# First weights and tables of five stages loaded in the stage before them, or by a second queue

## The chip, the core and the metric

The kernel runs on one core of a Trainium2 chip. All times are device microseconds of one execution; the time of a kernel is the median of several executions. Tensors are float32. The engines of the core are TensorE (PE in the rows; its weight loads are PEld), VectorE (DVE), ScalarE (ACT), GpSimd (POOL) and SyncE (SP). Transfers are issued by SP's queue, by ScalarE's (ACTq) and by GpSimd's; they run on 16 transfer engines.

## What is computed

One layer of a diffusion backbone over 2048 latent tokens of width 1024, with a context of 256 tokens ahead of them. Cut to what the change touches:

```python
h = rmsnorm(x) * (1 + sc1) + sh1
p = h @ w_in                                     # 1024 x N_IN
ya, _, _ = deltanet_branch(p[:, :A_COLS], ...)   # recurrence over chunks, two directions
x0, x1, v = split(short_conv(p[:, B_OFF:C_OFF]) + b)          # Hyena, 256 wide each
z = x1 * v
yb = x0 * (irfft(rfft(z, 4096) * rfft(kern, 4096))[:2048] + z * bias)
yc = B * short_conv(C * hx)                                   # from p[:, C_OFF:G_OFF]
gates = sigmoid(p[:, G_OFF:])                                 # 3 x 1024
merged = gates[0] * (ya @ w_branch_a) + gates[1] * (yb @ w_branch_b) + gates[2] * (yc @ w_branch_c)
x = x + g1 * (merged @ w_out)                                 # then norm, routing to experts, final norm
```

## The kernel before

The program is a chain of stages. Each is one `nc.Block()` with a list of instructions for each engine, and between two blocks all engines meet at a barrier; within a block they meet by semaphores (`then_inc`, `wait_ge`), and each engine takes its list in order. A transfer adds 16 to its semaphore when it has landed. Buffers that a stage allocates with `sbt(st, ...)` are given back at its end, so the next stage's buffers lie in the same bytes and can't be filled before the barrier. `recycle()` clears all semaphores and adds one more barrier. Between 685 and 1295 us runs the recurrence (DN here, block of line 1124); the stages behind it are those of the change:

- **H** (block of line 1543): projections and short convolutions of Hyena and of the short branch. Twelve quads `q` take a weight block `raw[:, q % 2]` (`raw_h`, 1024 KB, loaded by `load_raw`) and multiply it with half of `hT` in seven products of four matrices each (Winograd's form of a 2 x 2 product): line 1589, in the order `p1`, `p5`, `u2`, `c11`, `u3`, `c12`, `c21`. VectorE makes the sums of weights (`s1` to `s4`) and of tokens (`t1` to `t4`), ScalarE keeps intermediate results (`p1s`, `p5s`, `u2s`: `kept`, line 1655). Beside them ScalarE scales tiles of `ada_w` (`scale_tiles`, line 1661) and GpSimd adds them up (line 1879); six of these tiles come ahead of `p1s` in quad 0. SP issues `load_raw(0)`, `load_raw(1)`, ten rows of a few KB, and then the `ada_w` tiles (line 1556). `z` goes to memory as `z_d`; the filter `h_d` was written in the first stage.
- **A** (block of line 1896): first step of the transform. For 16 blocks of four columns SP loads four pieces `hb` (filters, 64 KB) and four `zb` (signal, 32 KB), up to four blocks ahead; TensorE multiplies with the table `fw`; VectorE copies to `az` (two buffers, 66 partitions), ScalarE's queue stores three parts of 264 KB to `fa_d`, and VectorE waits for these stores (`a_st`) before it fills the buffer again. SP loads `fw` in two parts, of 528 KB (behind block 0) and 1584 KB.
- **C** (block of line 1975): second step, products of the spectra and the inverse step. Eleven blocks `sp_in` (two buffers, six pieces of 192 KB each, reloaded when the block two earlier is used up); 22 parts, each with products by the matrices `gm` 0 and 1 (lines 2023, 2024, part `s = 0` of the block only), 2 to 5 (lines 2027 to 2030, parts 1 and 2) and 6 (line 2013). In between the recurrence's outputs are read (`load_o`, 512 KB a tile), added and normalised. Results go to `fb_d`.
- **D** (block of line 2127): last step. 16 blocks `bb` (two transfers of 132 KB, 66 rows) times the table `fd` (66 rows, 528 KB); both buffers have 128 partitions, and VectorE and GpSimd set the rows from 64 on to zero before the transfers may write. Each block is followed by four transposes of `yaT` (line 2168).
- **Y** (block of line 2209): y is loaded as `yn` (four transfers of 512 KB), transposed on TensorE, and multiplied on VectorE and GpSimd.
- **W** (block of line 2277): gates and branch products. 24 quads of the same seven products (line 2314), with weights `raw_w` (1024 KB a quad) and `bw` (1024 KB in three parts, used one quad later).

## Time and profile before

| | |
|---|---|
| time, median of 3 (us) | 4042.16 (4040.48 to 4047.41) |
| profiled execution: time, span (us) | 4042.21, 4040.4 |
| TensorE busy | 3744.9 us, 93% |
| VectorE, ScalarE, GpSimd busy | 48%, 27%, 22% |
| bytes moved | 384 MB read, 111 MB written, mean 122 GB/s |

The span is that of the profile, from the first to the last instruction; the time of the same execution is 1.8 us longer. In rows with a duration the first number is the start in us from the span's start, the second the length; brackets hold the idle time of the engine ahead of the row and what ended it. A row may join instructions of the same kind that follow one another (`x8`); a float32 matrix product shows as two records. The share of a transfer row and the clock are means over the stretch; the clock is 1.00 at 2.4 GHz and 0.50 at 1.2 GHz.

### The profile page before, as it was taken

To read this page: it belongs to the slowest core of one execution; us is meant where nothing else is said; L and a number is where in the kernel's file an instruction comes from. 1 tells how busy PE (TensorE), PEld (TensorE's weight loads), DVE (VectorE), ACT (ScalarE), POOL (GpSimd) and SP (SyncE) were. 2 spreads that over 40 slices of the span, in tenths; PEclk is the share of its full clock that TensorE was granted. 3 is DMA by queue.
4 is the path that set the end of the run, shared out by engine and by line. 5 is a ranking of instruction groups with operands and counts; after the bars stand their busy time and mean duration, and the time that the engine had idled before them with its cause. 6 is when DMAs were issued, how large, how long until landed. Compare 5 with 4: busy or idle time off the path is not lost. (4 is left out here: it accounts for less than half of the span.)

```text
span 4040.4 us, 46896 instructions
## 1 busy us (share of the span) xinstructions
PE 3744.9 (93%) x17200; PEld 2401.5 (59%) x17200; DVE 1942.1 (48%) x2964; ACT 1101.5 (27%) x2313; POOL 900.5 (22%) x661
## 2 busy tenths in 40 slices
PE   6999998999998999887999999997976999999997
PEld 2854444888887444344344444443546888888885
DVE  4344544555555743635322222224435666666667
ACT  4155555444444511031111111111210111111113
POOL 1012222333333700031011111111331222122224
PEclk8699999999999999988999999998977999999998
DMA  7122333222222511695111111105442655665565
GB/s 267 35 76 76 89 94 98 71 78 78 78 78 82 181 54 42 199 238 167 57 53 54 52 54 58 55 27 195 140 174 84 215 189 202 207 213 193 192 218 210
DMA packets 297697, 497.25 MB, mean 123 GB/s; under 512 B 21447, under 2 KB 176746, under 8 KB 297204
## 3 DMA queue, kind: packets, MB, share of 16 engines
q1 hardware_dynamic: 277601, 431.65, 32.3%
q0 software_dynamic: 12096, 43.84, 4.1%
q10 hardware_dynamic: 7829, 19.46, 1.5%
q8 instruction: 110, 1.80, 0.2%
q14 instruction: 61, 0.50, 0.0%
HBM read 384.11 MB, written 110.77 MB: 122 GB/s over the span
## 5 line engine op out<-in xcount | busy, mean ns | idle before, releaser
L2314 PE MATMUL bank<-hT,raw_w 128*128 128x512 f32 x576 | 260.6, 595 | 9.5 <-DMA raw_w<-in_w_in 9.5
L3343 PEld LDWEIGHTS bank<-xeT,raw_e 128*128 128x128 f32 x2304 | 263.6, 192 | 7.2 <-issue 7.2
L3343 PE MATMUL bank<-xeT,raw_e 128*128 128x128 f32 x2304 | 267.8, 275 | 0.0
L2506 POOL TENSOR_TENSOR mg<-mg,sg_m 128x512 f32<-128x512 f32 x64 | 88.1, 1377 | 719.3 <-DVE sg_m L2408 719.3
L887 POOL TENSOR_SCALAR sg<-tmp 128x512 f32<-128x512 f32 (+1 forms) x76 | 111.9, 1473 | 469.1 <-DVE tmp L955 413.9
L2314 PEld LDWEIGHTS bank<-hT,raw_w 128*128 128x128 f32 x576 | 110.0, 191 | 148.0 <-issue 138.2
L3343 PE MATMUL bank<-T_e,U 128*128 128x128 f32 x1536 | 176.7, 275 | 0.0
L664 PE MATMUL bank<-T_d,S_d 128*128 128x512 f32 x384 | 174.1, 603 | 0.0
L3343 PEld LDWEIGHTS bank<-T_e,U 128*128 128x128 f32 x1536 | 174.1, 192 | 0.0
L2314 PE MATMUL bank<-zT,S 128*128 128x512 f32 x384 | 172.6, 592 | 0.0
L2408 DVE TENSOR_TENSOR sg_m<-sg_m,bank 128x512 f32<-128x512 f32 x64 | 43.9, 686 | 242.2 <-PE bank L2326 242.2
L2377 ACT ACTIVATE sg_m<-sg_m 128x512 f32<-128x512 f32 x72 | 45.4, 630 | 395.3 <-DVE sg_m L2417 395.3
L1211 PE MATMUL bank<-T,Nc 128*128 128x128 f32 x864 | 137.1, 281 | 15.0 <-DVE T L1411 11.9
L1221 PE MATMUL bank<-E,TTm 128*128 128x128 f32 x864 | 146.5, 294 | 0.3
L1434 DVE TENSOR_TENSOR E<-bank,lv 128x256 f32<-128x256 f32 x216 | 91.6, 424 | 82.6 <-PE bank L1211 82.1
L1221 PEld LDWEIGHTS bank<-E,TTm 128*128 128x128 f32 x864 | 113.4, 191 | 27.0 <-issue 3.0
L3349 PE MATMUL bank<-raw_e,hid_e 128*128 128x512 f32 x288 | 128.9, 592 | 0.0
L2314 PEld LDWEIGHTS bank<-zT,S 128*128 128x128 f32 x384 | 73.0, 190 | 91.8 <-issue 91.8
L1211 PEld LDWEIGHTS bank<-T,Nc 128*128 128x128 f32 x864 | 114.5, 192 | 20.9 <-issue 17.9
L664 PEld LDWEIGHTS bank<-T_d,S_d 128*128 128x128 f32 x384 | 73.9, 195 | 89.3 <-issue 89.3
L1295 ACT ACTIVATE Tq<-T 128x256 f32<-128x256 f32 x216 | 89.1, 420 | 122.3 <-DVE T L1443 73.6
L664 PE MATMUL bank<-hT,raw_d 128*128 128x512 f32 x256 | 118.2, 605 | 0.0
(509 smaller groups left out, 7641.1 us busy)
## 6 DMA issues: line engine op xcount, KB each, us to landing
raw_e<-in_exp_w_gate SPq DMA_DIRECT2D x16, 3072.0 KB
raw_e<-in_exp_w_up SPq DMA_DIRECT2D x16, 3072.0 KB
raw_e<-in_exp_w_down SPq DMA_DIRECT2D x16, 3072.0 KB
raw_w<-in_w_in SPq DMA_DIRECT2D x24, 1024.0 KB, 5.3
raw_d<-in_w_in SPq DMA_DIRECT2D x16, 1024.0 KB, 5.9
fa_d<-az ACTq DMA_DIRECT2D x48, 264.0 KB
sp_in<-fa_d SPq DMA_DIRECT2D x66, 192.0 KB, 5.2
raw_h<-in_w_in SPq DMA_DIRECT2D x12, 1024.0 KB, 5.3
```

Source lines behind the costliest of these rows:

```text
L664: mm = pe.matmul(bank[:, :], lhs[:, k, :], rhs[:, k, :], start=first and k == 0, stop=k == 3, skip_group_check=not first)
L887: pool.tensor_scalar_max(sg[:, g % TB, 0:w], tmp[:, g % TB, 0:w], CLAMP).then_inc(clamp_ok, 1)
L1211: last = pe.matmul(b4(x)[:, h % 2, :], Nc[:, h, :], mixed(T, b, h, 1, 0), start=True, stop=True)
L1221: last = pe.matmul(b4(2 + x)[:, h % 2, :], TTm[:, h, :], E1[:, h, :], start=True, stop=True)
L1295: act.activation(Tq[:, 2 * x:2 * x + 2, :].rearrange("p h (n t b) -> p (h n) t b", t=2, b=b), mixed(T, b, 2 * x, 2, 1), ACT.Copy).then_inc ...
L1434: dve.tensor_tensor(E1[:, 2 * x:2 * x + 2, :], b4(x)[:, 0:2, :], lv[:, l, :].unsqueeze(1).to_broadcast([P, 2, P]), ALU.mult).then_inc(P_ok, 1)
L2314: mm = pe.matmul(bank[:, :], lhs[:, k, :], rhs[:, k, :], start=first and k == 0, stop=k == 3, skip_group_check=not first)
L2377: act.activation(sg[:, i, :], src, ACT.Sigmoid).then_inc(sg_ok[i], 1)
L2408: dve.tensor_tensor(dst, sg[:, i, :], O(q, i)[:, :], ALU.mult).then_inc(pr_ok[i], 1)
L2506: pool.tensor_tensor(mg[:, i, :], mg[:, i, :], sg[:, i, :], ALU.add).then_inc(add_ok[i], 1)
L3343: mm = pe.matmul(bank[:, f * P:(f + 1) * P], lhs[:, k, f * P:(f + 1) * P], rhs[:, k, :], start=fresh and k == 0, stop=k == 3, skip_group_c ...
L3349: mm = pe.matmul(bank[:, :], lhs[:, f, :], rhs[:, f, :], start=first and f == 0, stop=f == HF - 1, skip_group_check=not first)
```

## The change

- `raw_h` is allocated at the other end of SBUF (`side="right"`), ahead of DN, and its two first loads are issued in DN, behind the first eight keys, queries and values; SP waits for them at DN's end. The waits of quads 0 and 1 go, those of later quads count one load less.
- In A the first part of `fw` and the four `hb` pieces of block 0 are issued by ScalarE's queue; SP begins with `zb`. The table `gm` (448 KB), allocated at the other end, is loaded in A, behind the second part of `fw`, and SP waits for it at A's end.
- In C the pieces `s = 0` of a block keep the semaphore `s_in`, the four others get `hz_in`, for which TensorE waits between lines 2024 and 2027.
- In D `bb` and `fd` have 66 partitions, the memsets and their semaphore are gone, and `fd` is issued by ScalarE's queue.
- `raw_w` and `bw` are allocated at the other end ahead of Y, and the first two loads of `raw_w` and the first three of `bw` are issued in Y behind `yn`.

```diff
@@ -1064,6 +1064,11 @@
+        far = lambda stack, name, shape: stack.enter_context(nc.sbuf_tensor(name, shape, F32, side="right"))
+        hst = top.enter_context(ExitStack())
+        raw_h = far(hst, "raw_h", [P, 2, KD, 2 * P])
+        raw_h_in = sem("raw_h_in")
+
         with ExitStack() as st:
             NL = len(LEVELS)
             lv, pair = sbt(st, "lv", [P, NL, P]), sbt(st, "pair", [P, P])
@@ -1136,6 +1141,9 @@
                             sp.dma_start(pair[:, :], A["t_pair"]).then_inc(lv_in, 16)
                     for e in range(4):
                         load(0, e, values, ldv)
+                    for q in range(2):
+                        c0 = B_OFF + q * HW
+                        sp.dma_start(raw_h[:, q], A["w_in"][0, :, c0:c0 + HW].rearrange("(k p) c -> p k c", p=P)).then_inc(raw_h_in, 16)
                     def step(it, w, inverse, more):
                         es = (2 * w, 2 * w + 1)
@@ -1151,6 +1159,7 @@
                                 load(it, e + 4, values, ldv)
                     all_steps(sp, step)
+                    sp.wait_ge(raw_h_in, 32)
                     for q in range(4):
                         sp.wait_ge(o_st[q], 16 * (STEPS // 2 + 1))
@@ -1478,7 +1487,8 @@
         with ExitStack() as st:
-            raw, S1, S2, S4 = sbt(st, "raw_h", [P, 2, KD, 2 * P]), *[sbt(st, n, [P, 4, P]) for n in ("S1_h", "S2_h", "S4_h")]
+            raw = raw_h
+            S1, S2, S4 = [sbt(st, n, [P, 4, P]) for n in ("S1_h", "S2_h", "S4_h")]
@@ -1555,8 +1565,6 @@
                             b, k = divmod(t, KD)
                             sp.dma_start(md[t % RM], A["ada_w"][0, k * P:(k + 1) * P, 2 * D + b * 512:2 * D + (b + 1) * 512]).then_inc(md_in[t % RM], 16)
-                    load_raw(0)
-                    load_raw(1)
                     for b in range(NMOD):
                         sp.dma_start(mod_row(b), A["ada_b"][:, 2 * D + b * 512:2 * D + (b + 1) * 512]).then_inc(n2_in, 16)
                     for b in (4, 5):
@@ -1608,7 +1616,8 @@
                     for q in range(NQ):
                         p, kind = quads[q]
-                        pe.wait_ge(raw_in[q % 2], 16 * (q // 2 + 1))
+                        if q >= 2:
+                            pe.wait_ge(raw_in[q % 2], 16 * (q // 2))
                         if q >= 2:
                             pe.wait_ge(x_free, q - 1)
                         product(X(q), w(q, 0, 0), t(p, 0, 0), True).then_inc(p1_mm, 1)
@@ -1782,7 +1791,8 @@
                             dve.sem_inc(x_free, 1)
                     def s1(q):
-                        dve.wait_ge(raw_in[q % 2], 16 * (q // 2 + 1))
+                        if q >= 2:
+                            dve.wait_ge(raw_in[q % 2], 16 * (q // 2))
                         if q >= 1:
                             dve.wait_ge(p5_mm, q)
                         dve.tensor_tensor(S1[:, :, :], w(q, 1, 0), w(q, 1, 1), ALU.add).then_inc(s1_ok, 1)
@@ -1886,6 +1896,10 @@
         EV = NB + NB // 2
         NBLK = FN // NB
         RB = 4
+        hst.close()
+        mst = top.enter_context(ExitStack())
+        gm = far(mst, "gm", [P, 7, P])
+        g_in = sem("g_in")
         with ExitStack() as st:
             fw = sbt(st, "fw", [P, NBLK, NB, 2 * FK])
             zb = sbt(st, "zb", [P, RB, HW])
@@ -1899,13 +1913,13 @@
                     for i in range(NBLK):
                         if i >= RB:
                             sp.wait_ge(a_mm, (i - RB + 1) * EV)
-                        for buf, src in ((hb, h_d), (zb, z_d)):
+                        for buf, src in ((hb, h_d), (zb, z_d)) if i else ((zb, z_d),):
                             for n in range(NB):
                                 sp.dma_start(buf[n * FR:(n + 1) * FR, i % RB], src.rearrange("(a n) c -> n a c", n=FN)[i * NB + n]).then_inc(b_in[i % RB], 16)
-                        if i == 0:
-                            sp.dma_start(fw[:, 0:RB], A["t_fa"][:, 0:RB]).then_inc(fw_in[0], 16)
                         if i == 1:
                             sp.dma_start(fw[:, RB:NBLK], A["t_fa"][:, RB:NBLK]).then_inc(fw_in[1], 16)
+                            sp.dma_start(gm[:, :, :], A["t_g"]).then_inc(g_in, 16)
+                    sp.wait_ge(g_in, 16)
                 @block.tensor
                 def _(pe):
@@ -1940,6 +1954,9 @@
                 @block.scalar
                 def _(act):
+                    act.dma_start(fw[:, 0:RB], A["t_fa"][:, 0:RB]).then_inc(fw_in[0], 16)
+                    for n in range(NB):
+                        act.dma_start(hb[n * FR:(n + 1) * FR, 0], h_d.rearrange("(a n) c -> n a c", n=FN)[n]).then_inc(b_in[0], 16)
                     for i in range(NBLK):
                         act.wait_ge(a_ev, (i + 1) * EV)
                         for s in range(3):
@@ -1960,13 +1977,12 @@
         own = lambda t: yaT[:, :, t * P:(t + 1) * P]
         with ExitStack() as st:
-            gm = sbt(st, "gm", [P, 7, P])
             sp_in = sbt(st, "sp_in", [P, 2, 3, 3, HW])
             xs = sbt(st, "xs", [P, 2, 2, CW])
             yp = sbt(st, "yp", [P, 2, 2, CW])
             bk = sbt(st, "bk", [P, 2, CW])
             obb, sqb, ss = sbt(st, "obb", [P, 4, HEADS, P]), sbt(st, "sqb", [P, 2, HEADS, P]), sbt(st, "ss_o", [P, TILES, HEADS])
-            g_in, s_in = sem("g_in"), [sem("s_in0"), sem("s_in1")]
+            s_in, hz_in = [sem("s_in0"), sem("s_in1")], [sem("hz_in0"), sem("hz_in1")]
             BLOCKS = FK // 3
@@ -1989,9 +2005,8 @@
                             sp.wait_ge(sx_mm, 4 * n - 4)
                         for s in range(3):
                             for r in range(2):
-                                sp.dma_start(sp_in[r * FN:(r + 1) * FN, n % 2, s], fa_d[s, r, 3 * n:3 * n + 3, :, :].rearrange("k n c -> n k c")).then_inc(s_in[n % 2], 16)
-
-                    sp.dma_start(gm[:, :, :], A["t_g"]).then_inc(g_in, 16)
+                                sp.dma_start(sp_in[r * FN:(r + 1) * FN, n % 2, s], fa_d[s, r, 3 * n:3 * n + 3, :, :].rearrange("k n c -> n k c")).then_inc((hz_in if s else s_in)[n % 2], 16)
+
                     load_block(0)
                     load_o(0)
                     load_block(1)
@@ -2012,16 +2027,17 @@
                             pe.wait_ge(c_cp, m - 1)
                         pe.matmul(PS[6 + m % 2][:, 0:CW], gm[:, 6, :], yp[:, m % 2, 0, :], start=True, stop=True).then_inc(c_mm, 1)
-                    pe.wait_ge(g_in, 16)
                     for m in range(PARTS):
                         n, v = m // 2, m % 2
                         if v == 0:
-                            pe.wait_ge(s_in[n % 2], 96 * (n // 2 + 1))
+                            pe.wait_ge(s_in[n % 2], 32 * (n // 2 + 1))
                         sig = [sp_in[:, n % 2, s].rearrange("p k c -> p (k c)")[:, v * CW:(v + 1) * CW] for s in range(3)]
                         if m >= 1:
                             pe.wait_ge(sx_cp, 2 * m)
                         pe.matmul(PS[0][:, 0:CW], gm[:, 0, :], sig[0], start=True, stop=True)
                         pe.matmul(PS[1][:, 0:CW], gm[:, 1, :], sig[0], start=True, stop=True).then_inc(sx_mm, 1)
+                        if v == 0:
+                            pe.wait_ge(hz_in[n % 2], 64 * (n // 2 + 1))
                         if m >= 2:
                             pe.wait_ge(sp_pr, 2 * m - 2)
                         pe.matmul(PS[2 + 2 * v][:, 0:CW], gm[:, 2, :], sig[1], start=True, stop=False)
@@ -2111,16 +2127,17 @@
                         if 0 <= t < TILES:
                             pool.wait_ge(o_in[t % 4], 32 * (t // 4 + 1))
                             pool.tensor_tensor(own(t), own(t), obb[:, t % 4], ALU.add).then_inc(sum_ok, 1)
+        mst.close()
         if stop == 9:
             return
         with ExitStack() as st:
             RD = 4
-            bb = sbt(st, "bb", [P, RD, NB, HW])
-            fd = sbt(st, "fd", [P, FN, FR])
+            bb = sbt(st, "bb", [2 * FK, RD, NB, HW])
+            fd = sbt(st, "fd", [2 * FK, FN, FR])
             ys = sbt(st, "ys", [FR, 2, NB, HW])
-            pad_ok, fd_in = sem("pad_ok"), sem("fd_in")
+            fd_in = sem("fd_in")
             o_tr, ya_ok = sem("o_tr"), sem("ya_ok")
             BE = NB // 2
@@ -2133,10 +2150,7 @@
                         for r in range(2):
                             sp.dma_start(bb[r * FK:(r + 1) * FK, i % RD], fb_d[r, i * NB:(i + 1) * NB, :, :].rearrange("n k c -> k n c")).then_inc(d_in[i % RD], 16)
-                    sp.wait_ge(pad_ok, 1)
                     load(0)
-                    sp.wait_ge(pad_ok, 2)
-                    sp.dma_start(fd[0:2 * FK], A["t_fd"]).then_inc(fd_in, 16)
                     for i in range(1, RD):
                         load(i)
                     for i in range(NBLK):
@@ -2170,7 +2184,6 @@
                 @block.vector
                 def _(dve):
-                    dve.memset(bb[64:P, :, :, :], 0.0).then_inc(pad_ok, 1)
                     for i in range(NBLK):
                         b = i % 2
                         if i >= 2:
@@ -2185,13 +2198,9 @@
                             dve.scalar_tensor_tensor(own(i), PS[4 + i % 4][:, :].rearrange("p (h t) -> p h t", t=P),
                                                      cols[:, R_NG:R_NG + 1], szb[:, i % 4], ALU.mult, ALU.mult).then_inc(ya_ok, 1)
-                @block.gpsimd
-                def _(pool):
-                    pool.wait_ge(pad_ok, 1)
-                    pool.memset(fd[64:P, :, :], 0.0).then_inc(pad_ok, 1)
-
                 @block.scalar
                 def _(act):
+                    act.dma_start(fd[:, :, :], A["t_fd"]).then_inc(fd_in, 16)
                     for i in range(NBLK):
                         act.wait_ge(d_ev, (i + 1) * BE)
                         act.dma_start(y_d.rearrange("(a n) c -> a n c", n=FN)[:, i * NB:(i + 1) * NB, :], ys[:, i % 2]).then_inc(d_st[i % 2], 16)
@@ -2203,6 +2212,10 @@
         ost.close()
         recycle()
+        wst = top.enter_context(ExitStack())
+        raw_w, bw = far(wst, "raw_w", [P, 2, KD, 2 * P]), far(wst, "bw", [P, KD, 2 * P])
+        raw_in, bw_in = [sem("raw_in0"), sem("raw_in1")], [sem(f"bw_in{j}") for j in range(3)]
+        branch_weights = [(0, 4, "w_branch_a"), (4, 2, "w_branch_b"), (6, 2, "w_branch_c")]
         with ExitStack() as st:
             yn, ty = sbt(st, "yn", [P, NT, 4, HW]), sbt(st, "ty", [P, 2 * NT, TW])
             y_in, y_tr, y_ok, y_own = [sem(f"y_in{g}") for g in range(NT)], sem("y_tr"), sem("yt_ok"), sem("y_own")
@@ -2211,6 +2224,11 @@
                 def _(sp):
                     for g in range(NT):
                         sp.dma_start(yn[:, g], y_d[g * TW:(g + 1) * TW, :].rearrange("(j p) c -> p j c", p=P)).then_inc(y_in[g], 16)
+                    for q in range(2):
+                        c0 = G_OFF + q * D
+                        sp.dma_start(raw_w[:, q], A["w_in"][0, :, c0:c0 + 2 * P].rearrange("(k p) c -> p k c", p=P)).then_inc(raw_in[q], 16)
+                    for q, (k0, nk, name) in enumerate(branch_weights):
+                        sp.dma_start(bw[:, k0:k0 + nk, :], A[name][0, :, 0:2 * P].rearrange("(k p) c -> p k c", p=P)).then_inc(bw_in[q], 16)
                 @block.tensor
                 def _(pe):
@@ -2245,13 +2263,13 @@
         with ExitStack() as st:
-            raw, S1, S2, S4 = sbt(st, "raw_w", [P, 2, KD, 2 * P]), *[sbt(st, n, [P, 4, P]) for n in ("S1", "S2", "S4")]
+            raw = raw_w
+            S1, S2, S4 = [sbt(st, n, [P, 4, P]) for n in ("S1", "S2", "S4")]
             T1, T2 = [zT[:, x, :].rearrange("p (k t) -> p k t", t=TW) for x in range(2)]
             T4 = sbt(st, "T4", [P, 4, TW])
-            bw = sbt(st, "bw", [P, KD, 2 * P])
             p1s, p5s, u2s = [sbt(st, n, [P, TW]) for n in ("p1s", "p5s", "u2s")]
             sg, mg = sbt(st, "sg_m", [P, 4, TW]), sbt(st, "mg", [P, 4, TW])
-            raw_in, bw_in, mg_st = [sem("raw_in0"), sem("raw_in1")], [sem(f"bw_in{j}") for j in range(3)], [sem(f"mg_st{i}") for i in range(4)]
+            mg_st = [sem(f"mg_st{i}") for i in range(4)]
             s1_ok, s2_ok, s3_ok, s4_ok = [sem(n) for n in ("s1_ok", "s2_ok", "s3_ok", "s4_ok")]
             t1_ok, t2_ok, t3_ok, t4_ok = [sem(n) for n in ("t1_ok", "t2_ok", "t3_ok", "t4_ok")]
@@ -2287,10 +2305,6 @@
                         _, k0, nk, name = branch[j]
                         sp.dma_start(bw[:, k0:k0 + nk, :], A[name][0, :, cp * 2 * P:(cp + 1) * 2 * P].rearrange("(k p) c -> p k c", p=P)).then_inc(bw_in[j], 16)
-                    load_raw(0)
-                    load_raw(1)
-                    for q in range(3):
-                        load_bw(q)
                     for q in range(1, NQ + 1):
                         p, cp, j = quads[q - 1]
                         if q + 1 < NQ:
@@ -2504,6 +2518,7 @@
                         for i in range(4):
                             pool.wait_ge(pr_ok[i], q + 1)
                             pool.tensor_tensor(mg[:, i, :], mg[:, i, :], sg[:, i, :], ALU.add).then_inc(add_ok[i], 1)
+        wst.close()
         if stop == 12:
             return
         yst.close()
```

## Rows read from the trace of the kernel before

**Rows 1.** The page, busy time and its share of the span, by engine.
```profile
PE 3744.9 (93%) x17200; PEld 2401.5 (59%) x17200; DVE 1942.1 (48%) x2964; ACT 1101.5 (27%) x2313; POOL 900.5 (22%) x661
```
**Rows 2.** Waits of PE, whole span: us in total, times, longest us.
```profile
PE bank L2023 <- DMA sp_in<-fa_d: 19.4, 5, 17.0
PE bank L2160 <- DMA fd<-in_t_fd: 15.6, 1, 15.6
```
**Rows 3.** Transfers of the whole span: count, KB each, median us to landing.
```profile
raw_w<-in_w_in SPq DMA_DIRECT2D x24, 1024.0 KB, 5.3
...
kN<-kN_d SPq DMA_DIRECT2D x36, 256.0 KB, 2.8
```
**Rows 4.** Timeline of the start of H: start, us, engine, line.
```profile
1298.43 1.02 SPq L1548 DMA_DIRECT2D raw_h<-in_w_in  x2
...
1303.07 1.78 SPq L1556 DMA_DIRECT2D x0T<-in_ada_w  x4
...
1303.71 6.69 PE L1589 MATMUL bank<-hT,raw_h 128*128 128x512 f32 x8 [9.95 <-DMA raw_h<-in_w_in]
...
1310.24 7.03 PE L1589 MATMUL bank<-T_h,S_h 128*128 128x512 f32 x16
...
1312.23 0.57 ACT L1655 ACTIVATE p1s_h<-bank 128x512 f32<-128x512 f32 x1
```
**Rows 5.** H: stretch, busy by engine, then PE's clock, transfer share, GB/s.
```profile
1307.00:1310.00 3.00, 3.00 (x5) 1.20 (x4) 3.00 (x4) 1.47 (x3) 0.05 (x1) 0.54 1.04 380
```
**Rows 6.** The same view, a stretch of DN.
```profile
700.00:720.00 20.00, 19.99 (x149) 18.28 (x149) 10.00 (x23) 10.14 (x27) 1.84 (x2) 0.95 0.02 5
```
**Rows 7.** Timeline of the start of A.
```profile
1622.35 1.81 SPq L1904 DMA_DIRECT2D hb<-h_d  x4
...
1626.06 0.42 SPq L1906 DMA_DIRECT2D fw<-in_t_fa  x1
...
1630.25 1.97 PE L1919 MATMUL bank<-hb,fw 128*66 128x512 f32 x2 [15.04 <-DMA fw<-in_t_fa]
```
**Rows 8.** Waits from 1622 to 1726: VectorE for its stores in A.
```profile
DVE az L1935 <- DMA fa_d<-az: 10.4, 10, 2.1
```
**Rows 9.** Timeline of PE within A.
```profile
1680.98 1.17 PE L1919 MATMUL bank<-hb,fw 128*66 128x512 f32 x2 [2.21 <-DMA zb<-z_d]
```
**Rows 10.** Two stretches of A, columns as in group 5.
```profile
1656.00:1663.00 7.00, 7.00 (x23) 2.99 (x22) 5.04 (x9) 0.00 (x0) 0.00 (x0) 1.00 0.74 221
1677.00:1688.00 11.00, 8.79 (x24) 3.54 (x23) 5.85 (x10) 0.00 (x0) 0.00 (x0) 0.84 0.61 194
```
**Rows 11.** Timeline of C: its start, and a later wait.
```profile
1727.56 0.35 SPq L1994 DMA_DIRECT2D gm<-in_t_g  x1
...
1727.97 3.96 SPq L1992 DMA_DIRECT2D sp_in<-fa_d  x6
...
1737.70 1.62 PE L2023 MATMUL bank<-sp_in,gm 128*128 128x384 f32 x2 [17.02 <-DMA sp_in<-fa_d]
...
1740.39 1.49 PE L2027 MATMUL bank<-sp_in,gm 128*128 128x384 f32 x2
...
1777.29 0.91 PE L2023 MATMUL bank<-sp_in,gm 128*128 128x384 f32 x2 [1.01 <-DMA sp_in<-fa_d]
```
**Rows 12.** Timeline of the start of D.
```profile
1850.37 3.47 DVE L2173 MEMSET bb<- 64x4096 f32 x1 [6.00 <-PEq L1975]
...
1855.73 0.31 SPq L2139 DMA_DIRECT2D fd<-in_t_fd  x1
...
1862.14 3.62 PE L2160 MATMUL bank<-bb,fd 128*32 128x256 f32 x8 [15.58 <-DMA fd<-in_t_fd]
```
**Rows 13.** Timeline of the starts of Y and W.
```profile
1907.96 2.03 SPq L2213 DMA_DIRECT2D yn<-y_d  x4
...
1922.37 1.00 SPq L2283 DMA_DIRECT2D raw_w<-in_w_in  x2
...
1927.74 5.30 PE L2314 MATMUL bank<-hT,raw_w 128*128 128x512 f32 x8 [9.52 <-DMA raw_w<-in_w_in]
```

## Prediction

> **What bounds the kernel now.** I read the page first: TensorE is busy for 93% of the span [rows 1], so a change pays only where TensorE stands still, and what it doesn't do on TensorE is free elsewhere. Then I read the waits of TensorE, longest first [rows 2]: the two single waits of 17.0 us (for `sp_in`) and 15.6 us (for `fd`) are for transfers that begin only when their stage begins, and so are those of 15.04 for `fw` [rows 7], 9.95 for `raw_h` [rows 4] and 9.52 for `raw_w` [rows 13]. These 67 us are not what can be won: each holds the tail of the stage before and the barrier too. So I went to the timeline at each of the five places and read two things: when the stage's first instruction is issued (the barrier is past), and when TensorE begins. Only the stretch between them is open to this change: 5.3 us for `raw_h` (1298.43 to 1303.71) [rows 4], 7.9 for `fw` (1622.35 to 1630.25) [rows 7], 10.1 for `gm` and `sp_in` (1727.56 to 1737.70) [rows 11], 11.8 for `fd` (1850.37 to 1862.14) [rows 12], 5.4 for `raw_w` (1922.37 to 1927.74) [rows 13]; 40.5 us in all. For each I then ask what is late next. The price of a transfer: 256 KB land in 2.8 us and 1024 KB in 5.3 [rows 3], so 3.3 us per 1024 KB and 2.0 that don't depend on size.
>
> **Stage H (Hyena and short convolution, `raw_h`).** Its two first weights are loaded in the recurrence stage, 600 us earlier, and both issues and their waits go from H. Added to the recurrence: two transfers of 1024 KB on SP's queue, behind the first keys and values and ahead of all later loads and stores of that queue. From 700 to 720 us all queues together move 5 GB/s, so that queue has nothing to do [rows 6]; two transfers of 1024 KB take 2.0+6.6 = 8.6 us and are through well before 720. Cost 0; if the cover were missing it would be these 6.6 us once. SP's new wait for them at that stage's end is met long before.
> In H TensorE can begin at 1298.5, 5.2 us sooner. Its first two products need only weights and the sums of VectorE, but the third needs `p1s`, which ScalarE makes after it has scaled six `ada_w` tiles; now these are issued from 1303.07 behind 2 MB of `raw_h`, and `p1s` is begun at 1312.23 [rows 4]. With the two issues gone (1.02 us) the tiles are issued from 1302.0, and nothing stands ahead of them in the transfer engines. Six tiles hold 1.5 MB: the last is there at 1302.0+2.0+5.0 = 1309.0, scaled by 1309.6 (about 0.6 us each, as `p1s` of the same shape; the other five are done by then), and `p1s` is ready at 1310.2. The third product stood at 1313.7, the middle of the last of [rows 4] (two products of eight records in 7.03 us from 1310.24), and comes 3.5 us sooner. I take 3.3, since ScalarE itself moves by only 1312.23-1309.6 = 2.6 and TensorE meets it again at `u2s`. Bounds 2.0 (the tiles come only 2 us sooner) and 5.2 (all of it).
>
> **Stage A (first transform, `fw`, `hb`).** `fw` and the four `hb` pieces go to ScalarE's queue, which has nothing before its first store; SP begins with `zb`. SP now issues 9 transfers before TensorE can start, 0.45 us each, `fw` last at 1626.06, which lands 4.2 us later [rows 7]. On two queues the last one needed is issued at about 1622.35+0.42+1.81 = 1624.6; landing 2.5 to 4.2 us later gives 1627.1 to 1628.8, so TensorE starts 1.5 to 3.1 us sooner. Does that last? The stage runs close to its transfers: from 1656 to 1663 the transfer engines are busy 0.74 at 221 GB/s, VectorE waits 10.4 us in ten places for its own stores, and TensorE once waits 2.21 us for `zb` [rows 8 to 10]. The change puts `gm` (448 KB, 2.1 us at 221 GB/s) among the loads here, and SP's later loads move up by the five issues that left it, 2.3 us. I take 1.5; bounds -1.0 (2.1 us of `gm` and no more than 1.1 of the issue time) and 3.3.
> The stretch from 1656 to 1663 shows a share of 0.74 although stores hold VectorE up. The Trainium skill (DMA: Bandwidth & Descriptors, Why a DMA increments its semaphore by 16 and not by 1) says that a transfer uses the largest number of engines up to 16 that divides its outer sizes, so 11 for the 66 partitions of `az`; 0.74 is close to 11/16 and agrees. The same page (Issuing engines are not separate DMA queues) says that a second queue saves only the issuing time; by it A would gain 2.3 less 2.1, about 0.2, and that is the first rival below.
>
> **Stage C (spectral products, `gm`, `sp_in`).** `gm` is gone from the front of the queue: 0.41 us of issue and 448 KB. The first wait now asks for two of the six pieces of `sp_in`, the other four are asked for two matrices later. Issued from 1727.56 at 0.66 us each, the two are out at 1728.9 and land at about 1732.4 (384 KB; 3.5 us). TensorE does the two products of `gm` 0 and 1, which take 2.69 us at the half clock (1737.70 to 1740.39) [rows 11], to 1735.2. All six carry 1152 KB; `gm` and they, 1600 KB, landed 10.1 us after the first issue, 2.0 and then 5.1 us for 1000 KB, so six land at 1727.56+2.0+5.9 = 1735.5. `L2027` starts there, not at 1740.39: 4.9 us. Bounds 3.0 (the six land only 3 us sooner) and 5.6.
> Inside the stage TensorE waits four more times for `sp_in`, 1.01 us the longest, 2.4 in sum: 19.4 less 17.0 [rows 2, 11]. The four later pieces get 1.3 us more (the two products at full clock, half of 2.69), which is more than 1.01: 2.4 us gained, bounds 1.2 and 2.4. Late next is the sum of VectorE and POOL, which is there in time now. The added wait on `hz_in` holds back only TensorE's own later products.
>
> **Stage D (last transform, no pads).** VectorE's memset is 3.47 us, and SP waits for it; POOL's follows, and only then, 5.36 us into the stage, is `fd` issued, which lands 6.4 us later [rows 12]. After: ScalarE issues `fd` at 1850.4, SP `bb` at once. If `fd` again takes 6.4 us, TensorE starts at 1856.8, 5.3 us sooner; but it now shares the engines with four `bb` blocks instead of having one ahead. With all of their 1056 KB mixed into its 528 KB at the 221 GB/s of [rows 10], plus 2.0, that is 9.2 us, 1859.6, 2.5 sooner. These are the bounds; I take 4.1, nearer to the row that is of `fd` itself. The products then read 66 partitions instead of 128; their columns are as many, cost 0.
>
> **Stage W (gates and branch products, `raw_w`, `bw`).** The five loads (3 MB) are issued behind `yn` in the stage before, the y transposes, which ends with a product on POOL; SP waits for none of them there. `raw_w` 0 begins to move when `yn` (2 MB, issued from 1907.96) is in [rows 13]: 1907.96+2.0+6.6+3.3 = 1919.9, before the 1922.37 at which W begins; `raw_w` 1 follows at 1923.2 and `bw` at 1926.5, and neither is asked for before W's second quad. VectorE's first sum and TensorE start together at 1922.4: 5.3 us; all that follows depends on VectorE, which moves by the same. If SP were still issuing at that stage's end it would hold the barrier: bound 4.0.
>
> **Clock.** Before each start TensorE has stood still and is granted 1.2 GHz; in H the clock is back at about 1309.8 (mean 0.54 over 1307 to 1310) [rows 5], 6.1 us after its start. The gaps of 4 to 12 us that stay are still such gaps, so I give nothing for a clock that never falls. The same eight matmul records take 6.69 us in H and 5.30 in W [rows 4, 13], 1.4 apart by where the clock comes back; at five places that is about 3 us either way. Starts that come a little sooner may meet a longer cold stretch; I charge 1.0.
>
> **Sum.** 3.3 + 1.5 + 4.9 + 2.4 + 4.1 + 5.3 - 1.0 = 20.5 us. The profiled execution took 4042.2 (span 4040.4 and 1.8 around it), the same as the median of 4042.16. Forecast 4042.2 - 20.5 = 4021.7.
>
> **Rivals.** (1) Transfers bind in A and D: the second queue brings no bytes sooner, `gm` only makes A's queue longer. A -1.0, D 2.5, the start of C 3.0: the sum falls by 2.5+1.6+1.9 to 14.5, 4027.7. For it speak the store waits of [rows 8], against it that at the start of A the queue is bound by issuing.
> (2) The 3 MB behind `yn` reach the engines beside it and not after it. TensorE's transposes wait, up to 3 MB at 3.3 us per MB, 9.9 us, and W's gain turns into a loss of 4.6: 4031.6. Against it: one queue, and the issues of `yn` take 2.03 us ahead of the first of them [rows 13].
> (3) Slower: gaps in A. At 1680.98 one wait of 2.21 us was followed by a stretch at half clock; the clock's mean over the 11 us from 1677 to 1688 is 0.84, so 1.7 us of full speed were lost too [rows 9, 10]. Such a wait costs 3.9. With TensorE 3 us ahead and `gm` between the loads, A could have them in many of its 16 blocks. Six more (23 us) turn the whole gain round; with eight, 31 - 20.5 gives 4053. Against it: there is one of them in sixteen blocks now.
> (4) The change does little: each stage finds another late partner as in H, and only 7 us of the sum stay, 4035. TensorE's waits name no such partner in C, D and W.
>
> **Chances.** Forecast 0.70; (1) 0.16; (2) 0.06; (3) 0.03; (4) 0.05. A measurement of this kernel tells about 0.2%, 8.1 us, from no change. Faster by more than that 0.92, within it 0.05, slower 0.03. The bounds of the terms add up to 14 to 27 with the clock in them; not all fall on one side. The range goes from 4013 (gains of 27 and 2 more by the clock) to 4034, where (1) and (2) are inside and (3) and most of (4) are not.
>
> **What would show it.** In the trace after: TensorE's first instruction of H and of W within 0.2 us of SP's first; third product of H waiting for `p1s` by 1 to 2 us; first `L1919` 5 to 6 us behind the stage's first issue; no waits for `sp_in` over 0.2 us inside C, `hz` products 8 us behind its first issue; `L2160` 6.4 to 9.7 behind. I am wrong if A's length from first issue to the next stage's first does not shrink (105.2 us now), if D's start needs 10 us, or if waits for `zb` multiply.

## The result, and the profile after

The changed kernel takes 4054.93 us (median of 14 executions, 4049.61 to 4060.18), the kernel before it, run beside it on the same chips, 4044.99 (14 executions). The ratio is 1.0026 with an interval of [1.0018, 1.0034]: slower by 0.26%, 10 us. The forecast was 4021.7 and the range ended at 4034, so the forecast is wrong in sign. The profiled execution after took 4060.18 us, its span is 4057.8 against 4040.4. It is the slowest of its 14, 5.3 us above their median, and the profiled execution before (4042.21) lies 2.8 under its own, so that the two spans are further apart, by 17.4 us, than the medians.

Where the 17.4 us came from in these two spans is read from the timelines: each stage from its first issue, or its first instruction, to that of the next. The terms below add up to the difference of the spans.

| stretch | before | after | difference | forecast |
|---|---|---|---|---|
| up to H | 1298.43 | 1299.35 | +0.9 | 0 |
| H | 323.92 | 322.73 | -1.2 | -3.3 |
| A | 105.21 | 107.11 | +1.9 | -1.5 |
| C, to D's first instruction | 122.81 | 114.07 | -8.7 | -7.3 |
| D, to `yn` | 57.59 | 85.02 | +27.4 | -4.1 |
| Y, to W's first product | 19.78 | 14.55 | -5.2 | -5.3 |
| from W's first product | 2112.66 | 2114.97 | +2.3 | +1.0 for the clock |

Five of the seven terms came within 2.1 us of what was forecast. A missed by 3.4 us and D by 31.5, and D alone turns the result round. A timeline of D's start in the changed kernel (start, us, engine, line):

```profile
1843.26 12.22 SPq L2151 DMA_DIRECT2D bb<-fb_d  x10
1843.26 0.33 ACTq L2203 DMA_DIRECT2D fd<-in_t_fd  x1
...
1851.16 3.59 PE L2174 MATMUL bank<-bb,fd 66*32 66x256 f32 x8 [10.79 <-DMA bb<-fb_d]
```

TensorE begins 7.9 us after the stage's first issue; before it was 11.8 ([rows 12], 1850.37 to 1862.14). So the start gained 3.9 of the forecast 4.1. Then the eight products of a block and the four transposes behind them take 4.6 us, and go on taking that. The stretches of D in the changed kernel (busy time and count by engine, then the granted clock, the transfer engines' share, GB/s):

```profile
1851.00:1866.00 15.00, 14.84 (x39) 6.43 (x40) 6.32 (x9) 0.00 (x0) 0.00 (x0) 0.50 0.51 140
1866.00:1924.00 58.00, 58.00 (x152) 24.61 (x151) 26.18 (x38) 0.00 (x0) 0.00 (x0) 0.50 0.41 118
```

and two stretches of D in the kernel before:

```profile
1862.00:1866.00 4.00, 3.86 (x10) 1.53 (x11) 0.88 (x2) 0.00 (x0) 0.00 (x0) 0.50 0.44 110
1866.00:1900.00 34.00, 34.00 (x169) 16.99 (x168) 25.16 (x39) 0.00 (x0) 0.00 (x0) 1.00 0.83 239
```

TensorE is never idle from 1866 to 1924, and its clock stays at the lower level, 1.2 GHz, for the whole 73.6 us of D's products. In the kernel before, the same stage is at 2.4 GHz from about 4 us after its first product, and 34 us hold 169 matmul records, where 58 us hold 152 after. The groups of matmuls by line and form (count, busy us, mean ns of one), first `L2174` in the changed kernel:

```profile
L2174 PE MATMUL bank<-bb,fd 66*32 66x256 f32 x128 | 57.9, 634 | 10.8 <-DMA bb<-fb_d 10.8
```
and `L2160` in the kernel before:

```profile
L2160 PE MATMUL bank<-bb,fd 128*32 128x256 f32 x128 | 32.3, 398 | 15.6 <-DMA fd<-in_t_fd 15.6
```

The first eight records show that a product itself got no longer: 3.59 us with 66 partitions (the first timeline above), 3.62 with 128 [rows 12], both at the lower clock. What the change lost is the return of the clock. D's products took 40.9 us from first to last before and 73.6 after: 32.8 us more, less the 3.9 of the start and 1.5 at the stage's end.

The other stages in the changed kernel, in their order. The timeline of H's start:

```profile
1299.39 5.37 PE L1597 MATMUL bank<-hT,raw_h 128*128 128x512 f32 x8 [4.70 <-PEq L144]
...
1310.19 0.58 ACT L1664 ACTIVATE p1s_h<-bank 128x512 f32<-128x512 f32 x1
...
1310.91 3.67 PE L1597 MATMUL bank<-T_h,S_h 128*128 128x512 f32 x8 [2.72 <-ACT p1s_h L1664]
```

TensorE starts 0.04 us behind the stage's first issue instead of 5.28, and then waits 2.72 us for `p1s`, which is begun 10.84 us behind the stage's first issue; before it was 13.80 [rows 4]. The third product is 3.7 us sooner in the stage (11.56 against 15.27 behind its first issue). The timeline of A's start:

```profile
1622.08 0.38 ACTq L1957 DMA_DIRECT2D fw<-in_t_fa  x1
1622.49 2.15 ACTq L1959 DMA_DIRECT2D hb<-h_d  x4
...
1629.88 1.94 PE L1933 MATMUL bank<-hb,fw 128*66 128x512 f32 x2 [14.93 <-DMA hb<-h_d]
```
Its stretch ahead of the first product (busy by engine, clock, transfer share, GB/s):

```profile
1624.00:1630.00 6.00, 0.12 (x1) 0.15 (x2) 0.00 (x0) 0.00 (x0) 0.00 (x0) 0.50 0.96 247
```
And the waits of the whole stage (us in total, times, longest), VectorE for its stores and TensorE for `zb`:

```profile
DVE az L1949 <- DMA fa_d<-az: 9.9, 8, 2.4
...
PE bank L1933 <- DMA zb<-z_d: 5.8, 5, 2.0
```

Nothing came sooner: 7.80 us from the first issue to the first product, 7.90 before [rows 7], with the transfer engines 0.96 busy meanwhile. The store waits are what they were (9.9 us, 10.4 in [rows 8]). The timeline of C's start:

```profile
1729.19 3.96 SPq L2008 DMA_DIRECT2D sp_in<-fa_d  x6
...
1733.24 1.65 PE L2037 MATMUL bank<-sp_in,gm 128*128 128x384 f32 x2 [11.22 <-DMA sp_in<-fa_d]
...
1736.78 0.61 PE L2043 MATMUL bank<-sp_in,gm 128*128 128x384 f32 x1 [0.61 <-DMA sp_in<-fa_d]
```
and the waits within the stage for `sp_in`:

```profile
PE bank L2043 <- DMA sp_in<-fa_d: 2.0, 4, 0.9
```

4.05 us pass from the first issue to the first product, against 10.14 [rows 11]. The product with `gm` 2 (`L2043`, `L2027` before) begins 7.59 us behind the first issue, against 12.83. Four waits for `sp_in` stay, 2.0 us in sum; the first of them is the 0.61 us ahead of that product. The timeline of TensorE at W's start:

```profile
1942.83 6.47 PE L2328 MATMUL bank<-hT,raw_w 128*128 128x512 f32 x8 [3.97 <-PEq L2222]
```
and of SP's queue in the stage ahead of it:

```profile
1930.36 4.00 SPq L2229 DMA_DIRECT2D raw_w<-in_w_in  x2
```

W's first product follows the end of the stage before at once; the first eight records take 6.47 us instead of 5.30 [rows 13], 1.2 us more at the lower clock.

### The profile page after: what moved, and what is told of

It is laid out like the page before. It is cut to its first block and busy times, and to the rows that moved or that the text cites. A ratio compares the mean times of both kernels' runs of the same rounds, so it can differ in the third digit from the quotient of the medians.

```text
span 4057.8 us, 46903 instructions
## 1 busy us (share of the span) xinstructions
PE 3779.0 (93%) x17200; PEld 2412.3 (59%) x17200; DVE 1938.8 (48%) x2963; ACT 1101.3 (27%) x2313; POOL 895.4 (22%) x660
## 5 line engine op out<-in xcount | busy, mean ns | idle before, releaser
L1220 PE MATMUL bank<-T,Nc 128*128 128x128 f32 x864 | 137.5, 282 | 15.0 <-DVE T L1420 11.8
```

Of the source, the lines that this page charges most:

```text
L1220: last = pe.matmul(b4(x)[:, h % 2, :], Nc[:, h, :], mixed(T, b, h, 1, 0), start=True, stop=True)
```

## The experiments

Two explanations stood against each other for D. The clock doesn't rise because of the products: 66 partitions instead of 128. Or it doesn't rise because of the start: TensorE begins 11 us sooner, without a memset and in another order of transfers. After that the questions were whether such products can hold the higher clock if they are given it, how the effect depends on partitions and columns, and why A gained nothing.

**The pads back in the changed kernel.** The changed kernel with D's pads as they were; everything else stays.

```diff
-            bb = sbt(st, "bb", [2 * FK, RD, NB, HW])
-            fd = sbt(st, "fd", [2 * FK, FN, FR])
+            bb = sbt(st, "bb", [P, RD, NB, HW])
+            fd = sbt(st, "fd", [P, FN, FR])
...
+                    sp.wait_ge(pad_ok, 1)
...
+                    dve.memset(bb[64:P, :, :, :], 0.0).then_inc(pad_ok, 1)
```

> The changed kernel with the last transform's pads put back: fd and bb have 128 partitions again, VectorE and GpSimd set rows 64 to 127 to zero before the loads, fd still goes by ScalarE's queue. Theory rows (66 filled rows of the array, instead of 128, leave TensorE at 1.2 GHz all through D, although it never stands still): clock back at 1.00 within about 7 us of D's first product, 2.4 us a block instead of 4.6; D starts some 5 us later than without pads (memsets 3.5 and 1.8 us) and ends some 26 to 31 us sooner. Time about 4032, ratio to before 0.997. Rival transfers (D is slow because fd and bb come by two queues at once and share the engines): nothing but 5 us more of start, time about 4060, D's blocks still 4.6 us.

Measured: 4033.42 us (4031.24 to 4036.4, five executions), ratio 0.9969 [0.9957, 0.9982]. The pads are worth 21.5 us to the changed kernel (4054.93 to 4033.42). D in this kernel, in stretches with the columns as above:

```profile
1858.00:1863.00 5.00, 4.82 (x13) 2.14 (x14) 1.47 (x3) 0.00 (x0) 0.00 (x0) 0.50 0.18 41
1863.00:1868.00 5.00, 5.00 (x24) 2.43 (x22) 3.71 (x6) 0.00 (x0) 0.00 (x0) 0.93 0.69 216
```

The first product is at 1858.18, and in the stretch from 1863 the clock is back (0.93). The gains of the other stages are real, and D's is the loss.

**No pads, and nothing else.** The kernel before with 66 partitions in `bb` and `fd`, without the memsets and the waits for them. `fd` stays on SP's queue, behind the first block.

```diff
-            bb = sbt(st, "bb", [P, RD, NB, HW])
-            fd = sbt(st, "fd", [P, FN, FR])
+            bb = sbt(st, "bb", [2 * FK, RD, NB, HW])
+            fd = sbt(st, "fd", [2 * FK, FN, FR])
```

> The kernel before with one edit alone: bb and fd have 66 partitions, the two memsets and their waits are gone, fd stays behind the first bb block on SP's queue. Theory rows: D's start 5 us sooner, then 4.6 us a block at half clock, 16 blocks x 2.2 = 35 us longer; time about 4045 + 30 - 4 = 4070, ratio 1.006 to 1.008. Rival transfers: D's blocks stay at 2.4 us, time about 4040, ratio 0.999.

Measured: 4070.93 us (4069.19 to 4071.6, five executions), ratio 1.0061 [1.0047, 1.0075]: 25.3 us slower than the kernel before.

One long stretch of its D, and the group of its products:

```profile
1860.00:1932.00 72.00, 72.00 (x189) 30.66 (x188) 32.61 (x47) 0.00 (x0) 0.00 (x0) 0.50 0.43 122
```
```profile
L2158 PE MATMUL bank<-bb,fd 66*32 66x256 f32 x128 | 58.0, 634 | 10.3 <-DMA fd<-in_t_fd 10.3
```

The same 634 ns a record and the same clock of 0.50 throughout, without any of the change's other parts. What these two runs leave open is whether the 66 partitions or the start without a memset ahead of it keep the clock down.

**Products of 128 partitions ahead of D's.** Seven further products of 512 columns on full tiles, which TensorE works off while it waits for D's first tables. Their results aren't used.

```diff
                         if i == 0:
+                            for _ in range(7):
+                                pe.matmul(PS[7][:, :], eye[:, :], yaT[:, 0, 0:512], start=True, stop=True)
                             pe.wait_ge(fd_in, 16)
```

> The changed kernel with seven products of 128 rows, 128 columns and 512 moving columns (eye times yaT, into a bank that is overwritten later, result unused) ahead of D's first wait, while the loads are under way. They take 6 to 12 us and bring the clock back at D's start. Theory rows: the first D products after them run at full clock (0.22 us a record), then the clock falls again and the rest of D is at half, time 4 us below or above that of the changed kernel, 4051 to 4059. Rival slower reads (a product over 66 rows takes twice as long at any clock): 0.45 us a record at a clock of 1.00. Rival late start (the clock only never came back because D began cold): the clock stays at 1.00, D 30 us shorter, time about 4025.

Measured: 4024.07 us (two executions), ratio 0.9947 [0.9929, 0.9965]. TensorE's timeline at D's start, and two stretches of D:

```profile
1840.88 7.77 PE L2169 MATMUL bank<-yaT,eye 128*128 128x512 f32 x14 [2.93 <-PEq L1991]
1848.58 1.91 PE L2176 MATMUL bank<-bb,fd 66*32 66x256 f32 x8
```
```profile
1840.00:1847.00 7.00, 6.12 (x11) 2.85 (x12) 0.00 (x0) 0.00 (x0) 0.00 (x0) 0.72 0.52 127
1847.00:1887.00 40.00, 40.00 (x193) 19.53 (x192) 28.72 (x45) 0.00 (x0) 0.00 (x0) 1.00 0.80 225
```

The extra products take 7.77 us and end as the first block lands; the clock has risen under them. The products of 66 partitions then run at 2.4 GHz for 40 us, 1.91 us for eight instead of 3.59. So these products hold the higher clock when they get it, and don't bring it about. That leaves the start in play, since only what came ahead of D was altered here; the kernel with rows of zeros, below, settles it.

The Trainium skill (TensorE: Matmul & The Clock Gate, What's actually happening) puts the clock down to how busy TensorE has been of late. By that rule the clock of D in the changed kernel should have risen soon after 1851, since TensorE was busy without a gap for 58 us; the trace says otherwise, and the measurement decides. That the clock holds in D once it is up agrees with the rule.

The same kernel was timed again later beside others, with five executions:

> The changed kernel with seven extra products (eye by a block of hT, 128 rows, 512 columns) that TensorE works off ahead of D's first wait; the extra products leave no result that is used. The kernel is the one that was looked at once, now timed in more rounds beside the next three. If the clock of D's 66-row products hangs only on what TensorE did before them: about 4024 us, 31 us under the changed kernel (54 us of a look at 0.50 of the clock against 46.7 us), and under the kernel before by 19 to 23 us. If that one look was a lucky one and 66-row products can lose the clock within D: anywhere from 4024 to 4055.

Measured: 4021.51 us (4020.7 to 4025.13), ratio 0.9953 [0.994, 0.9965]. So the first two executions were no lucky ones.

**Rows of zeros that are loaded.** The changed kernel with 128 partitions in D again, but without the memset ahead of everything: `fd` brings its rows of zeros in its own transfer on ScalarE's queue, and each of the four buffers of `bb` gets its lower rows cleared on its own, just ahead of its first load.

```diff
-    fd = np.concatenate([dd.real, -dd.imag], 0)
+    fd = np.concatenate([dd.real, -dd.imag, np.zeros((P - 2 * FK,) + dd.shape[1:])], 0)
...
+                            sp.wait_ge(pad_ok, i + 1)
...
+                    for i in range(RD):
+                        dve.memset(bb[64:P, i], 0.0).then_inc(pad_ok, 1)
```

> The changed kernel with pads that cost less: the table t_fd has 128 rows with zeros from row 66 on, so fd is loaded whole by ScalarE's queue at once (1024 KB on all engines) and needs no memset; bb is set to zero by VectorE one buffer at a time, and each first load waits for its own buffer only (about 0.9 us for the first). Theory rows: full clock in D, first product about 7 us behind the stage's start, time about 4026 to 4030, 3 to 6 us below the kernel with both memsets. Rival transfers: 4055.

Measured: 4027.72 us (4025.86 to 4031.35, five executions), ratio 0.9956 [0.9943, 0.997]. D in stretches:

```profile
1851.00:1857.00 6.00, 5.37 (x14) 2.32 (x15) 2.05 (x3) 0.00 (x0) 0.00 (x0) 0.50 0.50 128
1857.00:1862.00 5.00, 5.00 (x25) 2.50 (x24) 3.59 (x7) 0.00 (x0) 0.00 (x0) 0.96 0.68 202
```

TensorE begins at 1851.63, 7.2 us behind the stage's first issue, as early as without pads (7.9), and the clock is back 6 us later. Cold, at the same point of the stage and in the same order of transfers, 128 partitions bring the clock back and 66 don't: it was the partitions and not the start. Two things come with the rows of zeros besides: the table is 1024 KB instead of 528, and VectorE clears the buffers. The larger table is not the cause, as the run with 64 columns below shows (1056 KB, the clock stays down). VectorE's clearing is in every D here whose clock came back from a cold start, and in none of those where it didn't. Against it as the cause speak C in the kernel before, where VectorE does nothing ahead of the cold first product and the clock is at 1.00 from 1744 to 1750, 6 us behind it, and the next run, where the same clearing with 96 partitions brought the clock back 10 us later; D with 128 partitions and no clearing at all was not run. Both halves can be had together, the early start and the clock, and rows of zeros do for it.

**96 partitions.** The changed kernel with 96 partitions, cleared and loaded in the same way, cold.

```diff
-            bb = sbt(st, "bb", [2 * FK, RD, NB, HW])
+            bb = sbt(st, "bb", [96, RD, NB, HW])
```

> The changed kernel, without warming products, with bb and fd of 96 partitions instead of 66: rows 66 to 95 are zero (table with zero rows, bb set to zero a buffer at a time). D starts at 1.2 GHz. Theory graded (the more rows of the array are filled, the sooner the clock comes back): the clock is back within D, perhaps later than with 128 rows, time 4026 to 4040. Rival (all 128 rows are needed): half clock through D, time about 4057.

Measured: 4033.06 us (4025.72 to 4036.79, six executions), ratio 0.9972 [0.996, 0.9983].

D in stretches from its first product, 1846.84:

```profile
1847.00:1855.00 8.00, 8.00 (x21) 3.06 (x19) 2.79 (x4) 0.00 (x0) 0.00 (x0) 0.50 0.54 145
1855.00:1863.00 8.00, 8.00 (x23) 3.72 (x23) 3.91 (x6) 0.00 (x0) 0.00 (x0) 0.50 0.51 140
1863.00:1893.00 30.00, 29.55 (x146) 14.70 (x145) 21.55 (x34) 0.00 (x0) 0.00 (x0) 1.00 0.76 213
```

The clock comes back at 1863, 16 us behind the first product, where 128 partitions took 4 to 6 us and 66 never did. So the partitions have a graded effect. The 16 us are those of the profiled execution, with a mean granted clock of 0.958 over the kernel; in the six executions this mean was 0.955 to 0.960 and the times 11 us apart, so the return may have come at other times in the others.

**66 partitions and 64 columns of weights.** The changed kernel, cold, with `fd` given twice side by side, so that each product fills twice the columns of the array; the second half of its output isn't used.

```diff
-                            last = pe.matmul(PS[e % 4][0:FR, ...], fd[:, i * NB + n, :], bb[:, i % RD, n, :],
+                            last = pe.matmul(PS[e % 4][0:2 * FR, ...], fd[:, i * NB + n, :], bb[:, i % RD, n, :],
```

> The changed kernel, without warming products, with 66 partitions, but fd's 32 columns stand twice side by side (64 columns, 1056 KB), so each product fills twice as many columns of the array; the second 32 rows of the result are not used. D starts at 1.2 GHz. Theory filled array (what raises the clock is how much of the array a product fills, rows times columns): the clock comes back in D, time about 4026 to 4032. Rival rows (only the number of partitions counts): half clock through D, time about 4057.

Measured: 4062.31 us (4058.47 to 4062.94, three executions), ratio 1.0041 [1.0026, 1.0056].

A long stretch of its D, and the group of its products:

```profile
1866.00:1915.00 49.00, 49.00 (x129) 25.49 (x129) 22.51 (x32) 0.00 (x0) 0.00 (x0) 0.50 0.46 139
```
```profile
L2175 PE MATMUL bank<-bb,fd 66*64 66x256 f32 x125 | 57.5, 641 | 13.6 <-DMA bb<-fb_d 13.6
```

Twice the columns bring nothing: the clock stays at 0.50, a record takes 641 ns. The larger table lands later, so D's products begin 10.7 us behind its first issue instead of 7.9; that is part of the 7 us by which this kernel is above the changed one. In these runs the partitions made the difference and the columns none.

**A on one queue.** The kernel with the extra products ahead of D, and in A the first block of `hb` and the first part of `fw` back on SP's queue. (Its further difference to the kernel before in A is the load of `gm`.)

```diff
-                        for buf, src in ((hb, h_d), (zb, z_d)) if i else ((zb, z_d),):
+                        for buf, src in ((hb, h_d), (zb, z_d)):
...
-                    act.dma_start(fw[:, 0:RB], A["t_fa"][:, 0:RB]).then_inc(fw_in[0], 16)
```

> The kernel with the seven warming products ahead of D, and in A the first block's hb and the first part of fw back on SP's queue in the old order; gm stays in A behind the second part of fw. Theory: the second queue brought nothing in A; first product 7.8 us behind the first issue, A's length within 1 us of that of the kernel with warming alone, time within 2 us of it, 4022 to 4027. Rival (the prediction's term): the first product 2 us later and the time 1.5 us longer.

Measured: 4026.17 us (4020.91 to 4027.85, five executions), ratio 0.9953 [0.994, 0.9967], against 4024.07 and 4021.51 with both queues. TensorE's first product follows the first issue by 7.83 us (1621.96 to 1629.79). With two queues it was 7.80 in the changed kernel, and 7.10 to 7.80, mean 7.44, in the eight profiles with both queues and A's tables loaded in A; with one queue it was 7.68 to 7.90 in three, mean 7.80. The timeline with one:

```profile
1621.96 1.71 SPq L1918 DMA_DIRECT2D hb<-h_d  x4
...
1629.79 1.97 PE L1935 MATMUL bank<-hb,fw 128*66 128x512 f32 x2 [14.96 <-DMA fw<-in_t_fa]
```

So the second queue brought the first product some 0.4 us sooner, where 1.5 to 3.1 were forecast. (The Trainium skill, DMA: Bandwidth & Descriptors, Issuing engines are not separate DMA queues, says that a second issuing engine saves only the time of issuing, which is usually small; the 0.4 us agree.) The stage's length was 107.5 us here; in the seven of those eight profiles whose stores are whole it was 103.9 to 107.1, mean 105.7. The 107.5 lie outside the 1 us that was expected around the kernel with the extra products (104.4 and 105.6 in its two profiles). The kernel before and the one with only the pads taken out, with one queue and no `gm` in A, had 105.2 and 106.0. So the queue may save 1.8 us and `gm` cost as much, as the first rival had it, but one profile with a scatter of 3 us among the others doesn't show it; A as a whole gained nothing.

**A's tables loaded in the recurrence stage.** The kernel with the extra products ahead of D, and `gm` and the first part of `fw` loaded with `raw_h`.

```diff
+                        sp.dma_start(gm[:, :, :], A["t_g"]).then_inc(raw_h_in, 16)
+                        sp.dma_start(fwa[:, :, :, :], A["t_fa"][:, 0:4]).then_inc(raw_h_in, 16)
```

> The kernel with the seven warming products ahead of D (66 rows kept), and gm and the first part of fw loaded in the recurrence stage beside raw_h, so that A loads nothing but its data and the second part of fw. Theory A-is-transfers (fw's 528 KB on ScalarE's queue share the engines with the first pieces, so A's first product came no sooner than before, 7.8 us behind the stage's first issue, and gm made the rest of A longer): first product 4.5 to 5 us behind the first issue, A from first issue to the next stage's 101 to 103 us instead of 105 to 107, time 3 to 4 us below the kernel with warming alone, about 4020. Rival issue (only the number of issues counts): start 7 us as before, no gain.

Measured: 4022.64 us (4017.76 to 4025.68, five executions), ratio 0.9942 [0.9929, 0.9956]. The timeline of A's start, and two later stretches of A:

```profile
1620.29 1.72 SPq L1923 DMA_DIRECT2D zb<-z_d  x4
...
1624.38 1.97 PE L1936 MATMUL bank<-hb,fwa 128*66 128x512 f32 x2 [11.24 <-DMA hb<-h_d]
```
```profile
1650.00:1680.00 30.00, 27.71 (x86) 11.55 (x85) 20.75 (x33) 0.00 (x0) 0.00 (x0) 1.00 0.68 215
1680.00:1715.00 35.00, 31.20 (x91) 12.67 (x90) 21.81 (x34) 0.00 (x0) 0.00 (x0) 0.95 0.58 180
```

TensorE begins 4.09 us behind the first issue, 3.6 sooner, and A is 104.8 us long, as before and not the 101 to 103 expected. The 3.6 us are given back between 1650 and 1715, where TensorE stands idle for 6.1 us at a transfer share of 0.58 to 0.68: A is bound by something that isn't the sum of its bytes.

**Each store of A in two.** The kernel with the extra products ahead of D; each store of the 66 partitions of `az` is issued as partitions 0 to 63 and 64 to 65.

```diff
-                            act.dma_start(fa_d[s]...[:, i * NB:(i + 1) * NB, :], az[:, i % 2, s]).then_inc(a_st[i % 2], 16)
+                            for lo, hi in ((0, 64), (64, 2 * FK)):
+                                act.dma_start(fa_d[s]...[lo:hi, i * NB:(i + 1) * NB, :], az[lo:hi, i % 2, s]).then_inc(a_st[i % 2], 16)
```

> The changed kernel with the warming products ahead of D and each store of A's result (66 partitions) issued as two, partitions 0 to 63 and 64 to 65. Theory that A is bound by the stores of its result, whose 66 partitions are served unevenly by the transfer engines: A shortens from 104 to 107 us to about 95 to 100, and the whole from 4024 to about 4017 to 4020. Rival, that A is bound by the sum of what it moves: A stays at 104 to 107, the whole at 4022 to 4027. Slower by 1 to 4 us if the added issues on ScalarE (48 of them, some 0.05 to 0.1 us each) delay its evictions.

Measured: 4017.58 us (4015.49 to 4023.77, five executions), ratio 0.9941 [0.9928, 0.9954]; 3.9 us under the same kernel with whole stores (4021.51, timed beside it). A is 99.4 us long, 6.2 less than there. (Of these, the profile gives back 3.5 in D: its products take 42.6 us from first to last instead of 39.1, with five waits of TensorE for VectorE, 3.3 us in sum, that the other profile doesn't have.) Each of the added issues took about 0.48 us on ScalarE's queue, not the 0.05 to 0.1 expected; ScalarE has nothing else to do in A, and this did no harm. Two stretches of A with stores in two:

```profile
1645.00:1675.00 30.00, 30.00 (x94) 12.77 (x93) 22.28 (x36) 0.00 (x0) 0.00 (x0) 1.00 0.86 235
1675.00:1708.00 33.00, 33.00 (x104) 14.21 (x103) 24.02 (x39) 0.00 (x0) 0.00 (x0) 1.00 0.79 205
```
and about the same two with whole stores, in the first profile of the kernel with the extra products:

```profile
1649.00:1679.00 30.00, 30.00 (x94) 12.86 (x93) 21.77 (x36) 0.00 (x0) 0.00 (x0) 1.00 0.69 218
1679.00:1712.00 33.00, 29.27 (x89) 11.76 (x88) 22.11 (x34) 0.00 (x0) 0.00 (x0) 1.00 0.68 210
```

TensorE has no gap any more, and the transfer engines' share is 0.79 to 0.86 instead of 0.68. A was bound by its stores of 66 partitions as they were issued, and not by the sum of its bytes. In the three kernels below that have the stores in two, A is 93.9 to 94.1 us long. The rule of the Trainium skill that the prediction cited (DMA: Bandwidth & Descriptors, Why a DMA increments its semaphore by 16 and not by 1: as many engines, up to 16, as divide the outer sizes, so 11 for 66 partitions and 16 for 64) fits these shares: 11 of 16 is 0.69. No view shows the engines one by one, and a split into two equal parts, which would tell the rule from the mere number of transfers under way, was not run.

**Extra products at every stage's start.** The kernel with A's tables loaded in the recurrence stage, and besides the seven ahead of D two to seven extra products at the ends and starts of H, A, C, D and Y.

```diff
+        def warm(pe, n, b):
+            for _ in range(n):
+                pe.matmul(PS[b][:, :], eye[:, :], hT[:, 0, 0:512], start=True, stop=True)
```

> The kernel with the warming products ahead of D and with gm and the first part of fw loaded during DN, plus three to seven further products of 512 columns, whose results aren't used, where TensorE stands idle ahead of a first product: at the ends and starts of H, A, C, D and Y. Theory that the low clock at the stages' starts is paid for in time: H's first 4 us, A's first 4 us and C's first 8 us ran at 0.50 to 0.59; half of each would be given back where TensorE is the engine that ends the stretch, 2 + 2 + 4, so that the time falls from 4022.6 to about 4015 to 4019. Rival: these starts are bound by DVE (H, all of 1304 to 1312 busy) and by transfers (A and C, transfer engines' share 0.9 to 1.1), so that a higher clock only makes TensorE wait: 4021 to 4025. Slower, up to 4030, where a warming product stands in the way of a block that had landed (each is 0.43 us at half clock).

Measured: eleven executions, seven between 4015.1 and 4025.8 and four between 4047.68 and 4053.8; median 4025.45, ratio 0.9966 [0.9945, 0.9987]. The median of the seven, 4018.96, is 3.7 us under the kernel without these products, but the kernel before, run beside each, was 2.3 us faster here (4042.43 against 4044.76), so that some 1.4 us are left of the 4 to 8 expected. The expectation took a product for 0.43 us at the lower clock; it is two records of 0.43 us each at the higher. The profiled one is of the four (4051.04). TensorE's timeline at its D, and two stretches:

```profile
1837.67 6.25 PE L2183 MATMUL bank<-yaT,eye 128*128 128x512 f32 x14 [1.20 <-PEq L2002]
1845.02 1.89 PE L2190 MATMUL bank<-bb,fd 66*32 66x256 f32 x8 [1.10 <-DMA bb<-fb_d]
```
```profile
1845.00:1849.00 4.00, 3.98 (x15) 1.93 (x16) 2.11 (x3) 0.00 (x0) 0.00 (x0) 0.75 0.78 193
...
1857.00:1917.00 60.00, 60.00 (x158) 25.99 (x158) 27.51 (x40) 0.00 (x0) 0.00 (x0) 0.50 0.40 117
```

This kernel comes to D with the higher clock, so that the same seven products are done after 6.25 us and TensorE stands idle for 1.1 us before the first block (and for 1.2 before the first extra product). The first eight products of 66 partitions still run at the higher clock, then it falls, and it stays down to the end of D. I read the four late executions as those in which this happened. The mean granted clock of each execution, which was recorded, fits: 0.957 to 0.959 in the four and 0.965 to 0.967 in the seven, and 0.008 of 4050 us is what some 65 us at half clock take from the mean.

**Extra products everywhere, and the stores in two.** The edits of the last two kernels together.

```diff
+                            for lo, hi in ((0, 64), (64, 2 * FK)):
...
+                    warm(pe, 4, 7)
```

> The two kernels of the warming products everywhere and of the split stores, put together. If their gains are in different stages, the sum of the two: 4022.6 less what each brought, at best 4010 to 4014. If A's stores gain nothing and the clock at the starts gains nothing: 4022 to 4025. If A becomes shorter by the split stores, TensorE's clock at A's start counts for more than in the kernel without them, 1 to 2 us beyond the sum.

Measured: 4011.81 us (six executions, five of them 4007.35 to 4012.95 and one 4041.14), ratio 0.9936 [0.9912, 0.996]. The profiled execution took 4012.3; its timeline at D:

```profile
1830.97 6.25 PE L2184 MATMUL bank<-yaT,eye 128*128 128x512 f32 x14 [1.20 <-PEq L2003]
1838.18 1.89 PE L2191 MATMUL bank<-bb,fd 66*32 66x256 f32 x8 [0.97 <-DMA bb<-fb_d]
```

The same extra products, the same idle time before them and a gap of 0.97 us behind them; here the clock held (the one late execution has a mean clock of 0.959, the other five 0.966 to 0.967): from the first extra product to D's last it is 46.2 us, and 79.2 in the kernel above. A is 93.9 us long, so that with the stores in two the earlier start of A and its clock count: 5.4 us less than with the stores alone.

**Two ways out of the chance.** Once the same with 128 partitions in D (as in the rows of zeros above) and no extra products ahead of it:

```diff
-                            for _ in range(7):
-                                pe.matmul(PS[7][:, :], eye[:, :], yaT[:, 0, 0:512], start=True, stop=True)
...
+                    for i in range(RD):
+                        dve.memset(bb[64:P, i], 0.0).then_inc(pad_ok, 1)
```

> The kernel of the warming products everywhere and the split stores, with D's products back at 128 partitions (fd carries rows of zeros, each buffer of bb has its lower rows set to zero ahead of its own load) and without the seven warming products ahead of D. Theory that the late executions (4041 and 4048 to 4054 us beside 4007 to 4025) are those in which the clock falls in the gap ahead of D's first products and 66-row products then never raise it: with 128 rows the clock comes back within 4 to 7 us, all executions lie within 8 us of each other, and the median is 4010 to 4016, D's products beginning 7 us behind its first issue. Rival, that the late executions come from something else (another stage's clock, a transfer): they stay, some 1 in 3 to 1 in 6, about 30 us above the rest.

Measured: 4013.38 us (4010.83 to 4015.4, five executions), ratio 0.9925 [0.9912, 0.9939]. It is faster than the kernel before, run beside it, by 30 us, and its median is some 42 us under that of the changed kernel. Its ratio is the best of the study, but within the interval of the kernel above, whose median without the late execution is 4011.33. D in stretches:

```profile
1838.00:1843.00 5.00, 5.00 (x18) 2.20 (x17) 2.23 (x4) 0.00 (x0) 0.00 (x0) 0.68 0.42 109
1843.00:1848.00 5.00, 5.00 (x27) 2.51 (x25) 4.07 (x7) 0.00 (x0) 0.00 (x0) 1.00 0.86 244
```

D's products begin 7.5 us behind its first issue, at 1837.59, and the clock is back before 1843. And once with 66 partitions and twelve extra products, so that no gap is left ahead of the first block:

```diff
-                            for _ in range(7):
+                            for _ in range(12):
```

> The kernel of the warming products everywhere and the split stores, with twelve instead of seven warming products ahead of D, so that TensorE isn't idle between the last of them and the first product of 66 rows (0.97 to 1.10 us idle before). Each is 0.45 us at full clock: the five more add 2.2 us of work, of which 1.0 fills the gap and up to 1.2 delays D. Theory that the gap ahead of the 66-row products is where the clock is lost: no execution about 30 us above the rest, median 4009 to 4013. Rival, that it is lost in the gap ahead of the warming products (1.20 us) or in D itself: late executions stay, 1 in 3 to 1 in 6.

Measured: 4018.21 us (4010.75 to 4019.65, five executions), ratio 0.9931 [0.9918, 0.9945]. TensorE's timeline at D:

```profile
1832.43 10.54 PE L2184 MATMUL bank<-yaT,eye 128*128 128x512 f32 x24 [1.21 <-PEq L2003]
1842.90 1.91 PE L2191 MATMUL bank<-bb,fd 66*32 66x256 f32 x8
```

The median missed the 4009 to 4013 expected by 5 us. The expectation took an extra product for 0.45 us, but that is one of its two records: 24 records take 10.54 us where 14 took 6.25, so the five more cost 4.3 us, of which 1.0 fills the gap, and D's products begin 10.5 us behind the stage's first issue instead of 7.3.

No late execution in either. With late ones at 5 in 17 (four of eleven and one of six), none in ten would come by chance about 3 times in 100, and none in the five of either kernel 17 times in 100. For the closed gap the other runs say more. In the four kernels with seven extra products ahead of D and none elsewhere, TensorE went from them to the products of 66 partitions with no idle time in the profile, and their 22 executions (seven, five, five and five) have none that is late. With the five here, that is none in 27 without a gap against 5 in 17 with one of about 1 us. If the gap made no difference, all five would fall among the 17 about 6 times in 1000. That points at the gap ahead of D's first product; but the four kernels also begin their extra products at the lower clock, and only the one with twelve differs from the late ones in the gap alone. That 128 partitions remove the risk rests on five executions and is likely, not shown.

## Why the prediction was wrong

**The step that failed** is the last sentence of the part on D: "The products then read 66 partitions instead of 128; their columns are as many, cost 0." The duration of a product was right (3.59 against 3.62 us for eight at the same clock). Its effect on the clock was not asked. The part on the clock then took over, for all five starts, the return that [rows 5] show for H, 6.1 us after the start; those are products of 128 partitions. For D with 66 partitions no row of before shows a return. That effect should have been bounded like the other costs that the trace of before doesn't show, and one end of the bound could be worked out: never back, so that D's 40.9 us of products, 4 of them at the lower clock, take some 37 more. That is more than the whole sum and would have stood as the slower rival; 32.8 were measured, a block taking 4.6 us instead of 2.4, which is less than twice. The slower rival that stood there (gaps in A) did not happen: A's waits for `zb` grew only to 5.8 us in five places, and the clock from 1677 to 1688 was 1.00 against the 0.84 of [rows 10].

The rows of before hold nothing that has 66 partitions. A's products are `128*66` [rows 7], with 66 columns and all 128 partitions, and their clock came back [rows 10]; the prediction, which looked at columns alone, could have asked of its own rows what the clock does with fewer partitions, and found that they don't say.

**H**: forecast 3.3. The mechanism was right: TensorE 5.2 us sooner, then a wait for `p1s`, which came 3.0 us sooner by ScalarE. The stage's length is 322.7 in the profile after and 319.1 to 323.3, mean 321.5, over the ten kernels that have this part and no extra products in H; without it 323.9 and 324.0. So 2.4 us, inside the bounds of 2.0 and 5.2. The third product itself came 3.7 us sooner; where 1.3 of it went was not followed.

**A**: forecast 1.5, measured nothing (105.7 against 105.6, the means given above). The first rival was right here in its reason: the second queue saves issues, and at A's start the transfer engines are at 0.96, so the first product came only some 0.4 us sooner. Beyond that the forecast and the rival both missed what binds A: its stores of 66 partitions. The prediction had the sign of it in hand, the share of 0.74 beside 11/16, and drew nothing from it.

**C**: forecast 4.9 at the start, for the product with `gm` 2 (`L2027` before), and 2.4 inside. That product begins 7.59 us behind the first issue in the changed kernel and 7.6 to 8.2, mean 7.85, over the ten profiles with the new C and no extra products in it, against 12.83 and 12.80 with the old: 5.0 on average and 5.2 in the pair, as forecast and by the mechanism forecast. (The first product of all gained more, 6.1 us; about 1 us of it is given back ahead of that product.) From there to the last product it is 103.6 us in the changed kernel and 103.9 on average of the ten, against 106.2 and 105.2: 1.8 inside instead of 2.4, since waits for `sp_in` stayed where the prediction allowed none over 0.2 us. Together 6.8, against the forecast of 7.3; the pair of profiles in the table gives 7.8.

**D's start**: forecast 4.1, measured 3.9.

**W**: forecast 5.3, measured 5.2; and the clock's charge of 1.0 is the 1.2 us that W's first eight records took longer (5.2 to 6.7 us over the profiles without extra products in Y, by where the clock comes back). With the extra products in Y, W's products take 798.1 us from first to last in three kernels and 799.8 in the fourth, instead of 800.9 in the changed one.

With D's products left out, the terms measured sum to 2.4 + 0 + 6.8 + 3.9 + 5.2 - 1.2 = 17.1 us. To them comes 0.9, which the prediction didn't have: from C's last product to D's first instruction it is 3.81 us where D begins with the memset over all buffers, and 2.88 where it doesn't. The kernel with the rows of zeros, which has all of this, gained 18.0 (4045.68 beside it, 4027.72). That the two agree to the tenth is luck, since A and H alone scatter by 3 to 4 us from profile to profile. The one with the old pads, which lacks D's start and the 0.9, gained 12.3. So the forecast of 20.5 was some 2 too high without the step that failed, and the failure is one step of 32.8 us.

One sum of the prediction is wrong: the lower bounds of its terms (2.0, -1.0, 3.0, 1.2, 2.5 and 4.0) add up to 11.7, and to 10.7 with the clock's charge, not to 14. The range ended at a gain of 8, so it held them all the same.

**Still open**: whether the partitions of the streamed rows or those of the loaded weights made the difference; in all kernels here both have the same number. Why the clock fell in one execution after gaps of 1.2 and 1.1 us and held in another after 1.2 and 1.0, no trace here tells. Whether 128 partitions bring the clock back in D without any clearing by VectorE, and what else than the number of engines could have made the stores in two faster, was not run.

## What to carry to other kernels

A clean-up that makes the matmuls of a stage use fewer partitions can cost the stage its clock, even where no product gets longer and TensorE is never idle: compare the granted clock of the stretch, and ask for each stage that begins cold (TensorE idle before it, at the lower clock) whether its own products bring the clock back. Rows of zeros that come in with the load, or a few full products ahead of it, cost TensorE nothing where it waits anyway. The full products were the faster of the two by 3.65 us (4024.07 and 4027.72, run beside each other), but between them and the stage's own products TensorE must not stand idle: late executions came only where such a gap stood. The full rows are the safer, since they bring the clock back themselves. And a stage whose transfer engines show a share well below 1 while its stores are waited for may be bound by an awkward number of partitions, not by bytes: a second queue and earlier loads did next to nothing for A's length, splitting the store took 6 us off.

## What the runs showed of the hardware

- Products of 66 partitions, with full transposes between them and no idle time, stayed at 1.2 GHz for 73.6 us; begun at 2.4 GHz they stayed there for 40 us. Cold, 96 partitions had the clock back after 16 us in the one execution profiled, 128 after 4 to 6 us in four kernels. 64 instead of 32 columns of weights changed nothing. Rows of zeros are enough for it.
- A fall within such a stage was not made good: in one profiled execution some 70 us at 0.50 from a fall 2 us after the first product, about 30 us in the time. Late executions came only where about 1 us of idle time stood ahead of the first such product: 5 of 17 with it, none of 27 without.
- With stores of 66 partitions, waited for, the transfer engines' mean share was 0.68 to 0.69; with the same stores split into 64 and 2 it was 0.79 to 0.86 and the stage 6 us shorter.
